# Gated-delta stage: matmuls of the opening by direction on four pairs of banks, last own blocks negated by VectorE, first decays behind the inverses

## What is computed

```
cum = jnp.cumsum(g, axis=-1)                       # inside a chunk
diff = cum[..., :, None] - cum[..., None, :]
d_incl = jnp.exp(jnp.where(incl, diff, -jnp.inf))
a_mat = beta[..., :, None] * einsum('nhcid,nhcjd->nhcij', k, k) * d_strict
gam = jnp.exp(cum)
sol = triangular_solve(a_mat, rhs, lower=True, unit_diagonal=True)
p_intra = einsum('nhcid,nhcjd->nhcij', q, k) * d_incl
# step over chunks: u = u0 - w S;  o = q_g S + p u;  S = g_end S + k_d^T u
```

## Time and profile before

| | us |
|---|---|
| median of three runs | 3769.05 (3767.85 to 3771.04) |
| the profiled execution | 3769.02 |
| its span | 3767.2 |
| TensorE busy | 3479.3 (92%) |
| VectorE busy | 2253.2 (60%) |
| ScalarE busy | 1242.9 (33%) |
| mean granted clock of TensorE | 0.97 of full speed |

### The profile page before, as it was taken

The page is one execution under the profiler, slowest core; times in us unless marked ns, Lnnn a source line. Parts: engine busy times, 40 slices in busy tenths (PEclk is TensorE's granted clock), DMA queues, the critical chain, the costliest instruction groups (busy, mean ns, idle before and its releaser), DMA issues. The chain is left out here.

```text
span 3767.2 us, 65830 instructions
## 1 busy us (share of the span) xinstructions
PE 3479.3 (92%) x27928; PEld 2122.7 (56%) x27928; DVE 2253.2 (60%) x3987; ACT 1242.9 (33%) x2181; POOL 282.0 (7%) x233
## 2 busy tenths in 40 slices
PE   7788988989999888888989998999999997999999
PEld 4367436676644467545766644666666664444444
DVE  3575467876652476457976754476666667433453
ACT  3353354534431254254634532121221221321002
POOL 0010100000000010000000000222222221000000
PEclk9899999999999999999999998999999998999999
DMA  4334112220053323312220042111111102213221
GB/s 168 106 88 137 53 34 84 78 102 11 10 188 111 100 88 100 95 43 79 80 105 9 10 151 82 35 46 40 46 46 40 45 18 84 84 50 112 89 95 45
DMA packets 302163, 281.51 MB, mean 75 GB/s; under 512 B 18208, under 2 KB 274592, under 8 KB 301872
## 3 DMA queue, kind: packets, MB, share of 16 engines
q1 hardware_dynamic: 301872, 277.30, 22.9%
HBM read 203.93 MB, written 73.33 MB: 74 GB/s over the span
## 5 line engine op out<-in xcount | busy, mean ns | idle before, releaser
L3456 DVE SCALAR_TENSOR_TENSOR cv<-glu,params,cv 128x1024 f32<-128x1024 f32 x240 | 361.0, 1504 | 6.4
L1492 PE MATMUL ps<-hT,w_cols 128*128 128x512 f32 x576 | 253.5, 600 | 8.1 <-PEq L160 8.1
L413 PE MATMUL ps<-hT,w_cols 128*128 128x512 f32 x448 | 196.0, 595 | 1.6 <-PEq L160 1.6
L1492 PEld LDWEIGHTS ps<-hT,w_cols 128*128 128x128 f32 x576 | 110.5, 192 | 146.3 <-issue 144.3
L3752 PE MATMUL ps<-hT,wr 128*128 128x512 f32 x360 | 161.7, 593 | 0.0
L413 PEld LDWEIGHTS ps<-hT,w_cols 128*128 128x128 f32 x448 | 84.3, 190 | 109.1 <-issue 109.1
L3432 POOL TENSOR_TENSOR Sp<-Sp,Rp 128x520 f32<-128x520 f32 (+1 forms) x56 | 88.5, 1580 | 565.5 <-DVE W L3473 565.5
L3215 PE MATMUL ps<-hT,w_f 128*128 128x347 f32 x384 | 116.2, 462 | 5.3 <-DMA w_f<-in_w_in 5.3
L3230 PE MATMUL ps<-w_i,hT 128*128 128x128 f32 x1024 | 120.7, 278 | 0.0
L3230 PEld LDWEIGHTS ps<-w_i,hT 128*128 128x128 f32 x1024 | 116.1, 192 | 2.2 <-issue 1.6
L3752 PEld LDWEIGHTS ps<-hT,wr 128*128 128x128 f32 x360 | 68.5, 190 | 86.0 <-issue 86.0
(11 more groups left out here) (930 smaller groups left out, 7147.7 us busy)
## 6 DMA issues: line engine op xcount, KB each, us to landing
w_cols<-in_w_in SPq DMA_DIRECT2D x32, 512.0 KB, 3.9
wr<-in_w_in SPq DMA_DIRECT2D x24, 512.0 KB, 5.2
hT_hbm<-hT SPq DMA_DIRECT2D x2, 4096.0 KB, 13.9
hT<-hT_hbm SPq DMA_DIRECT2D x2, 4096.0 KB, 15.4
fh<-hT_hbm SPq DMA_DIRECT2D x16, 512.0 KB, 4.7
fh_again<-hT_hbm SPq DMA_DIRECT2D x16, 512.0 KB, 4.6
x<-in_x SPq DMA_DIRECT2D x8, 512.0 KB, 8.4
ahead<-kb_hbm SPq DMA_DIRECT2D x16, 256.0 KB, 3.4
```

Source lines behind the costliest of these rows:

```text
L413: q = pe.matmul(ps[:, proj_bank(n, b), :], lhsT=wc[:, n % 3, k, :], rhs=hT[:, k, P + b * 512:P + (b + 1) * 512], start=(k == 0), stop=(k = ...
L1492: q = pe.matmul(ps[:, proj_bank(n, b), :], lhsT=wc[:, n % 3, k, :], rhs=hT[:, k, P + b * 512:P + (b + 1) * 512], start=(k == 0), stop=(k = ...
L3456: vec.scalar_tensor_tensor(out=cv[:, h % 2, :], in0=src, scalar=w, in1=cv[:, h % 2, :], op0=ALU.mult, op1=ALU.add).then_inc(*VEC(f"tap{h}_ ...
```

## The change

The opening, that is everything ahead of `gam0` in `TURNS`, uses all four pairs of banks in turn, and `claim` looks four places back there (also for the first two users behind it). Both kinds of `pairs` and of their multiplications go by direction: n = 0 is all six heads forward, n = 1 all six backward, six matmuls and 768 elements each. `key_pairs(s, n)` waits only for its own direction's `DT` and copies, for which ScalarE marks `x{s}_0` behind the fifth piece. `values_in(0)` now waits for `AT3_0` and `fill(0)` for `AT3_1`, whose banks they take over. In the opening VectorE makes the forward copy into `AT6` (`across_blocks`); in rounds 3 and 7 it also negates the backward own blocks (`own_blocks`) instead of ScalarE. VectorE's `decays(0)` moves from ahead of `inverses(0)` to behind it. ScalarE's pieces in the middle loop are cut at slightly different places.

```diff
--- before.py
+++ after.py
@@ -1685,11 +1685,15 @@
                     for s in range(4, NT):
                         TURNS += ([f"gam{s + 1}"] if s < NT - 1 else []) + [f"kt{s}", f"q{s}_0", f"q{s}_1", f"o{s}"]
 
+                    FRONT = TURNS.index("gam0")
+
                     def pair_of_banks(name):
-                        return 2 * (TURNS.index(name) % 2)
+                        return 2 * (TURNS.index(name) % (4 if TURNS.index(name) < FRONT else 2))
 
                     def used_before(name):
-                        return TURNS[TURNS.index(name) - 2] if TURNS.index(name) > 1 else None
+                        at = TURNS.index(name)
+                        back = 4 if at < FRONT + 2 else 2
+                        return TURNS[at - back] if at >= back else None
 
                     begin("gdn_chunk")
                     with nc.Block() as block:
@@ -1718,6 +1722,8 @@
                                 if k0 == 0:
                                     pe.wait_ge(*DMA.upto("fw", n // NT + 1))
                                     pe.wait_ge(*DMA.upto(f"fh{n % 2}", n // 2 + 1))
+                                    if n == 0:
+                                        pe.wait_ge(*VEC["AT3_1"])
                                     if n == NT:
                                         pe.wait_ge(*ACT["w2_3"])
                                         pe.wait_ge(*VEC["w2_3"])
@@ -1740,11 +1746,10 @@
                             def pairs(s, n, of):
                                 name = f"{'q' if of == 0 else 'g'}{s}_{n}"
                                 b = claim(name)
-                                for em in range(4 * n, 4 if n == 0 else 6):
-                                    e, m = em // 3, em % 3
+                                for m in range(3):
                                     for h in range(2):
                                         c0 = slice(64 * h, 64 * h + 64)
-                                        q = pe.matmul(ps[:, b + h, P * (em % 4):P * (em % 4) + P], lhsT=gq[c0, 3 + m, tok(s, e)], rhs=gq[c0, of + m, tok(s, e)],
+                                        q = pe.matmul(ps[:, b + h, P * m:P * m + P], lhsT=gq[c0, 3 + m, tok(s, n)], rhs=gq[c0, of + m, tok(s, n)],
                                                       start=True, stop=True)
                                 q.then_inc(*PE(name))
 
@@ -1765,6 +1770,8 @@
                                 q.then_inc(*PE(f"gam{s}"))
 
                             def values_in(s):
+                                if s == 0:
+                                    pe.wait_ge(*VEC["AT3_0"])
                                 for em in range(6):
                                     e, m = em // 3, em % 3
                                     for h in range(2):
@@ -1861,6 +1868,8 @@
                             def join(b):
                                 pe.wait_ge(*VEC[f"RX{b}"])
                                 pe.wait_ge(*ACT[f"x{4 * b + 3}_1"])
+                                if b == 0:
+                                    pe.wait_ge(*VEC["AT6_3"])
                                 for hf in range(2):
                                     at = claim(f"pc{b}_{hf}")
                                     for n in range(12):
@@ -1953,7 +1962,9 @@
                                             c.then_inc(*ACT(f"G{s}_{e}"))
                                     elif p < 6:
                                         q = e + 2 * (p - 4)
-                                        act.copy(AT5[rows(q), n, :], AT[rows(q), u, beside(q)])
+                                        c = act.copy(AT5[rows(q), n, :], AT[rows(q), u, beside(q)])
+                                        if p == 5 and p1 == 6:
+                                            c.then_inc(*ACT(f"x{s}_{e}"))
                                     else:
                                         near, far = (HIGH, LOW) if e else (LOW, HIGH)
                                         act.copy(AT6[near, s % 4, :, :], AT[near, u, far]).then_inc(*ACT(f"x{s}_{e}"))
@@ -2028,13 +2039,11 @@
                                 if s < 3:
                                     decay_pairs(s + 1, 0)
                                 if s < 3:
-                                    take_out(s, 0, 0, 7)
+                                    take_out(s, 0, 0, 6)
                                     decay_pairs(s + 1, 1)
                                     take_out(s, 1, 0, 7)
                                 else:
-                                    take_out(s, 0, 0, 4)
-                                    take_out(s, 1, 0, 4)
-                                    take_out(s, 0, 4, 7)
+                                    take_out(s, 0, 0, 6)
                                     take_out(s, 1, 4, 7)
                             decays(0)
                             for n in range(NT - 1):
@@ -2049,15 +2058,14 @@
                                 decays(s + 1)
                                 first_half(s)
                                 if s:
-                                    take_out(s + 3, 0, 4, 6)
+                                    take_out(s + 3, 0, 4, 5)
                                 decay_pairs(s + 4, 0)
                                 across(s)
                                 if s:
-                                    take_out(s + 3, 0, 6, 7)
-                                    take_out(s + 3, 1, 0, 1)
+                                    take_out(s + 3, 0, 5, 7)
                                 second_half(s)
                                 if s:
-                                    take_out(s + 3, 1, 1, 4)
+                                    take_out(s + 3, 1, 0, 4)
                                 decay_pairs(s + 4, 1)
                                 if s:
                                     take_out(s + 3, 1, 4, 7)
@@ -2069,7 +2077,6 @@
                                 else:
                                     take_out(s + 4, 0, 0, 4)
                                     out(s)
-                                    take_out(s + 4, 1, 0, 4)
                                     take_out(s + 4, 0, 4, 7)
                                     take_out(s + 4, 1, 4, 7)
                             for n in range(NT, 2 * NT - 1):
@@ -2109,18 +2116,17 @@
                                 q.then_inc(*VEC(f"DTb{s}_{e}"))
 
                             def of_heads(ap, n):
-                                return ap[:, 8 * n:8 if n == 0 else 12, :].rearrange("p (u h) n -> p h u n", h=2)
+                                return ap[:, 6 * n:6 * n + 6, :].rearrange("p (u h) n -> p h u n", h=2)
 
                             def pair_bank(name, n):
                                 b = pair_of_banks(name)
-                                return ps[:, b:b + 2, 0:512 if n == 0 else 256].rearrange("p h (u n) -> p h u n", n=P)
+                                return ps[:, b:b + 2, 0:3 * P].rearrange("p h (u n) -> p h u n", n=P)
 
                             def key_pairs(s, n):
                                 vec.wait_ge(*PE[f"g{s}_{n}"])
-                                if n == 0:
-                                    vec.wait_ge(*VEC[f"DTb{s}_1"])
-                                    if s:
-                                        vec.wait_ge(*ACT[f"x{s - 1}_1"])
+                                vec.wait_ge(*VEC[f"DTb{s}_{n}"])
+                                if s:
+                                    vec.wait_ge(*ACT[f"x{s - 1}_{n}"])
                                 vec.tensor_tensor(of_heads(AT, n), pair_bank(f"g{s}_{n}", n), of_heads(DT[:, s % 5], n), ALU.mult).then_inc(*VEC(f"AT{s}_{n}"))
 
                             def query_pairs(s, n):
@@ -2183,8 +2189,17 @@
                                                   ps[:, pair_of_banks(f"o{s}") + 1, 0:GW].rearrange("p (u n) -> p u n", n=GD), GD ** -0.5, None,
                                                   ALU.mult).then_inc(*VEC(f"o{s}"))
 
+                            def own_blocks(s):
+                                vec.wait_ge(*VEC[f"AT{s}_1"])
+                                if s > 4:
+                                    vec.wait_ge(*PE["of0_1"])
+                                for q in range(4):
+                                    c = vec.tensor_scalar(G[rows(q), 1, :, 18:24], AT[rows(q), 6:12, rows(q)].rearrange("p u i -> p i u"), -1.0, None, ALU.mult)
+                                c.then_inc(*VEC(f"G{s}_1"))
+
                             def inverses(b):
-                                vec.wait_ge(*ACT[f"G{4 * b + 3}_1"])
+                                vec.wait_ge(*ACT[f"G{4 * b + 3}_0"])
+                                vec.wait_ge(*VEC[f"G{4 * b + 3}_1"])
                                 for e in range(2):
                                     vec.transpose(Zl[:, e].rearrange("p i c -> p (i c)"), G[:, e].rearrange("p i n -> p (i n)")).then_inc(*VEC(f"Z{b}_{e}_0"))
                                 for j in range(1, 31):
@@ -2228,17 +2243,23 @@
```

(13 more changed lines are left out.)

## The result

The changed kernel takes 3749.6 us (median of four, 3748.96 to 3753.35); the kernel before 3769.67 (median of four, 3767.85 to 3771.04). The ratio is 0.9949 with an interval of 0.9933 to 0.9965. So it is 20.1 us faster, where 22.9 were forecast (3746). The profiled execution took 3750.07 us.

The account below looks back on a forecast made before the run. A loop of waits between VectorE, ScalarE and TensorE was taken to bound the gated-delta stage's opening. 10.5 + 0.5 + 0.45 = 11.4 us a layer, 22.9 in two, took 3769 to 3746 us; eight-in-ten range 3739 to 3756.

Parts of the forecast that it names:

- main case: Whole kernel: 3746 us, within 3743 to 3751, chance 0.55.
- Part 1: Opening by directions on four pairs of banks: ScalarE's 7.95 us a round bounds it, last key_pairs ends at 568.95, not 573.62.
- Part 2: Ahead of inverses(0): last own blocks to VectorE (1.25 us), its decays(0) moved behind; transposition near 570.3, inverses ready at 605.6.
- The new wait: fill(0) waits for AT3_1: fillings start at 569.0, lose 1.9 us to low clock, and start the join at 607.3, 10.5 earlier.
- Rival (a): TensorE's clock holds: fillings end at 605.4, inverses decide the join at 605.6; 13.7 us a layer, 3742 us, chance 0.25.
- Part 3: Rest of the stage: 0.5 us off the first join without idleness ahead (bounds 0 and 1.3), plus 0.45 ahead of inverses(1).
- The second join: VectorE's wait for ScalarE's negations ahead of inverses(1) shrinks: 0.45 us earlier, counted in full, bound 0.
- The middle loop: Pieces only change sizes: round 0 gains about 0.6 us, rounds 1 to 3 cost about 0.2 each; sum 0, bounds -1 and +1.
- The late loop: After the middle loop: 0, its first pairs shorter by what the second is longer, TensorE without gaps.
- (b): TensorE bounds the opening at low clock, 9.2 us a round: only the tail is gained, 3758 us, chance 0.12.
- (c): Gain taken back later, or waits don't part as written: under 3.7 us a layer, about 3764, chance 0.05.
- (d): Slower: low clock doesn't end in the fillings; with four more at half rate 3788 us, chance 0.03.

Follow-up runs that it names:

- late_decays: The changed kernel with TensorE's values_in(0) ahead of decays(0), so that decays(0) runs just before fill(0): 3757.71 us.
- mid_pe: The changed kernel with TensorE's keys_on_state(s + 1) ahead of pairs(s + 4, 1) in the middle loop: 3758.66 us.
- own_act: The changed kernel with the backward own blocks of rounds 3 and 7 negated by ScalarE again: 3749.32 us.
- mid_act: The changed kernel with one of ScalarE's four middle-loop negations moved behind the exponential of decay_pairs(s + 4, 1): 3752.66 us.
- early_fill_timed: The changed kernel with the opening's last two pairs on the first banks, fillings without the AT3_1 wait, TensorE's decays(0) behind fill(0): median 3753.88 us of nine.
- best2: The changed kernel with two pairs of banks, no added waits, fill(0) ahead of TensorE's decays(0), both middle-loop edits: median 3749.17 us of six.

## Why the prediction was right, and where it was off

**The bound, the chain and the sign were right.** The loop of 8.83 us a round was the release of `AT`, and the first join was the point to follow. Of the sum of 11.4 us a layer, 9.6 and 10.5 came, and 3749.6 us lies in the main case. Part of this nearness is luck: the terms behind the join missed by up to 2 us in single layers and cancelled.

**Part 1, the opening.** The last `key_pairs` was forecast to end 33.9 us behind the start (568.95) and did at 34.1; ScalarE's list of 7.95 us a round was the bound, as `key_pairs` of one direction at 567.50 and 575.59 show (8.1 apart). That distance is seen only in the last round; before it VectorE's own list sets the pace, 6.9 us a round, while ScalarE falls behind. (The prediction calls the rounds of 554.14 and 562.97 the second and third, which are s = 1 and 2, and the exponential of 544.08 that of the second direction; it is the first one of round 1. The sum uses the right times.) The copy into `AT6` took 0.34 to 0.35 us (0.4 taken). But I gave the freedom to two causes, the banks and the release. Beside the release the banks had no part in it: with two pairs the opening was the same to 0.4 us, and with the joint release and four pairs it was 6 to 7 us longer (in the new order of VectorE's list). What two pairs would do under the joint release in that order was not run. My sentence that TensorE stood still because only two pairs were in use read the releaser of its waits (the earlier trace rows and the rows near it name line 2124) as the cause; it was the same loop seen from TensorE.

**Part 2, own blocks and decays.** The price was right (1.30 for 1.25 us, four times 0.33 with no overlap), the transposition came at 35.6 (35.2 forecast). The move of `decays(0)` is worth 2 us at the join and was hidden behind the inverses as said. The own blocks are worth nothing there, which follows from my own two ends (fillings 607.3, inverses 605.6): I had the numbers and did not say it.

**The new wait.** That the fillings and not the inverses would decide, and that the low stretch moves onto `fill(0)`, held: clock 0.50 over the first 4.7 us, fillings of 38.96 and 38.63 us up to the join for 38.3 forecast. The term was undersized: 2.5 and 2.2 us for the 1.9 that I took. I had taken a low stretch of 4.2 us; the granted clock stood at 0.50 for 5.3 us of the fillings in the first layer and 4.7 in the second, and half of that is the loss. The swap of one line that parts the idleness (late_decays) is what shows it to be the clock. The Trainium skill (TensorE: Matmul & The Clock Gate, "What's actually happening") says that an array left idle drops to 1.2 GHz and comes back once it has been busy; the trace agrees, with 3.46 us of idleness ahead of the stretch at 0.50. With this, the join gained 9.5 and 9.8 us for 10.5. Rival (a), the clock that holds, is what two pairs of banks would have given: 71.3 and 70.9.

**Part 3, the join's inside.** I took 0.5 us; measured -0.2 and +2.4 us. From the join to the first `right_side` the profiles have 13.2 to 16.5 us in most runs whose fillings decide the join (18.2 in the first layer of mid_pe) and 14.5 to 19.1 in those whose inverses decide it, TensorE being idle right ahead. The two groups overlap. By layer one sees more: in the first layers they don't differ (15.8 to 18.2 us where the fillings decide, 14.6 to 17.7 where the inverses do), in the second ones they nearly part (13.2 to 13.8, once 15.5, against 14.5 to 19.1). So the 2.4 us of the second layer, 2.6 in the other pair of unchanged kernels, may be the idleness ahead that went, more than my bound of 1.3, but no run parts it from the rest. What makes the length shows in the rows: stalls without a releaser, and the low clock. In the changed kernel's first layer (clock 0.89) there were the stall of 1.73 us and then a half filling of 4.54 us for 2.85; its second layer (1.00) has one such idleness of 0.59 us, and took 2.95 us less.

**The second join.** Forecast 0.45 us earlier, measured none (54.3 to 54.4 us behind the fourth `right_side` in all four layers). The own blocks did bring 0.75 there (own_act), but the last `pairs` and `key_pairs`, each 0.2 to 0.3 us longer, and the 0.23 of the twelve products, took it away. I counted the 0.27 of `key_pairs` and left out the other two.

**The middle loop.** Forecast 0, measured 0.57 and 0.56 us lost a layer: round 0 gained 0.4 (0.6 forecast), rounds 1 and 2 lost 0.5 each, where I had 0.2. Half of that is the longer `pairs` on the state's path, as counted; the other half is VectorE's wait of 0.23 us for an exponential that ScalarE now does behind four negations instead of three. Taking this wait away (mid_act) gave 0.18 us a round back; that the rest is the `pairs` is argued, not shown. It was in the diff, in the shifted ends of `take_out`, and I named those ends without pricing them.

**The late loop and the rest.** Forecast 0; 0.4 and 0.1 us lost from the fifth to the eighth `right_side`. Second join to fifth `right_side`: 1.3 gained and 1.0 lost. All terms together, measured: 9.5 - 0.2 - 0.6 + 0 + 1.3 - 0.4 = 9.6 and 9.8 + 2.4 - 0.6 - 0.1 - 1.0 - 0.1 = 10.4.

Rivals (b), (c) and (d) did not come about: the granted clock of the opening was 0.88 (0.81 before), the gain was not taken back later, and the low stretch ended 5.3 us into the fillings. But the sentence against (d), that the longest low stretch of the trace is about 4 us, misread the trace of the kernel before. Ahead of the stage, with TensorE busy a third of the time, it has one of 20 us:

```profile
160.80:181.10 20.30, 6.95 (x32) 5.28 (x32) 9.97 (x19) 4.86 (x15) 6.47 (x9) 0.50 0.74 217
```

## What to carry to other kernels

When an engine is named as the releaser of several waits, undo each suspected cause by itself before crediting it: here undoing the separate release for each half of a buffer took two thirds of the gain away, and the extra banks cost 1.9 us at the first join, by where they let `decays(0)` run. When a chain is shortened, work out at once which parallel branch is late next; parts of the change that shorten the other branch are then worth nothing, and a wait put ahead of a long run of matmuls is paid twice, as idleness and as low clock behind it. Where one program differs by several us between executions, judge an edit by distances inside its stage in the profile, and a candidate only by the median of many executions.

## What the runs showed that I had not expected

- A single execution of a changed kernel can be 15 us below the median of the same program (3739.1 against 3753.9, nine executions from 3741.7 to 3764.2). Also the kernel before ranged from 3759.05 to 3777.57 in one set of 14.
- TensorE has stalls of 0.9 to 3.7 us that end without a releaser, nearly always in the same few places where many small matmuls follow each other (lines 977, 912 and 992 of the RWKV stage, 864, and the joining matmuls), but of a different length each time: nine in the profile of before, 14.7 us together, nine of 17.0 us after, twelve of 23.3 us in the last combination, counting those over 0.9 us. The DMA records of the profiles show what goes ahead of their end. The page has a queue "q8 instruction", with 222 packets of 16384 bytes; the second row is the queue around before's stall that ended at 1768.46, from 1765 to 1769:

```profile
q8 instruction: 222, 3.64, 0.4%
...
q8 instruction: 1, 0.02, 1.8%
```

  That packet had landed at 1767.05. In the fourteen profiles together there are 132 such stalls, and 129 of them end 1.05 to 1.6 us after a packet of this queue has landed; the other three, of 0.9 to 1.3 us, lie in fillings, with no landing within 8 us. So TensorE seems to stand there for its own instructions, and in the second layers of early_fill_timed and best2 the earlier first join met such a stall, of 3.4 and 3.7 us. No run changed how instructions arrive, so this is read from times and not tested.
- Moving a 1.5 us piece of work so that it ended 2.0 us ahead of a long run of matmuls, instead of 5.2 us, made that run 2.3 to 2.6 us shorter, by the granted clock alone.
